# A four-layer decoder trunk in one kernel: the norms between its stages, and one table request, put in another order

## What is computed

```python
for i in range(DEPTH):                       # 2
    hn = rms_norm(h, gains[0])
    mix = retention(hn, ...) if i % 2 == 0 else gated_deltanet(hn, ...)
    h = h + rms_norm(mix, gains[1])
    ff = square(relu(rms_norm(h, gains[2]) @ w_up)) @ w_down      # 1024 -> 4096 -> 1024
    h = h + rms_norm(ff, gains[3])
```

## Time and profile before

| | us |
|---|---|
| median of 3 runs (lowest, highest) | 1483.14 (1481.12, 1483.98) |
| the profiled execution's own time | 1481.87 |
| its span, first instruction to last | 1480.1 |
| TensorE busy | 1453.2 (98%) |
| GpSimd busy | 655.5 (44%) |
| VectorE busy | 591.6 (40%) |
| ScalarE busy | 546.0 (37%) |
| TensorE's granted clock, mean share of full speed | 0.993 |

### The profile page before, as it was taken

How to read it: one execution, slowest core, us unless ns; L and a number is a source line. 1 busy time by engine, 2 the same in 40 slices (tenths; PEclk the granted TensorE clock), 3 DMA queues, 4 the chain that set the end, 5 groups by cost and what they waited for, 6 DMA issues and landing times.

```text
span 1480.1 us, 19872 instructions
## 1 busy us (share of the span) xinstructions
PE 1453.2 (98%) x7772; PEld 1220.5 (82%) x7773; DVE 591.6 (40%) x1095; ACT 546.0 (37%) x1039; POOL 655.5 (44%) x306
## 2 busy tenths in 40 slices
PE   8999999999999999999999999999998999999998
PEld 6988888757889888888888977889988988888886
DVE  3641001264265520044037445797756640024223
ACT  5232243254243222222225457754734322123231
POOL 6245344343544353444447216357435444434442
PEclk9999999999999999999999999999999999999999
DMA  6322322400233223323232222221113132232321
GB/s 220 127 86 85 105 93 88 165 3 29 90 111 116 86 85 103 97 85 114 86 114 86 89 87 86 86 83 35 57 57 129 58 100 99 88 110 87 106 94 57
DMA packets 66557, 136.23 MB, mean 92 GB/s; under 512 B 3632, under 2 KB 4016, under 8 KB 66096
## 3 DMA queue, kind: packets, MB, share of 16 engines
q1 hardware_dynamic: 64016, 125.90, 25.8%
q10 hardware_dynamic: 2464, 9.25, 1.7%
HBM read 133.03 MB, written 2.11 MB: 91 GB/s over the span
## 4 chain that ended last, share of the span: by engine, by line
PE 90%; DVE 4%; ACT 3%; POOL 2%; DMA 1%; issue 1%; DVEq 0%; ACTq 0%; SPq 0%; POOLq 0%
PE bank L452 27%; PE bank L453 27%; PE bank L454 27%; PE bank L660 2%; POOL side_lo L331 1%; PE bank L774 1%; PE bank L646 1%; PE bank L730 1%; POOL w_lo L331 1%; DVE mix L1610 1%; DVE gv L1837 1%; ACT squares L1351 1%; PE bank L499 1%; DVE act_lo L1652 0%; DMA gains<-in_norm_gains_dram 0%
## 5 line engine op out<-in xcount | busy, mean ns | idle before, releaser
L331 POOL TENSOR_TENSOR w_lo<-w_raw,w_hi 128x1024 fp32r<-128x1024 f32 (+1 forms) x218 | 521.5, 2415 | 679.1 <-ACT w_hi L1050 676.2
L1050 ACT ACTIVATE w_hi<-w_raw 128x1024 fp32r<-128x1024 f32 x208 | 209.1, 1055 | 467.1 <-PE bank L454 424.5
L452 PE MATMUL bank<-act_hi,w_hi 128*128 128x512 f32 (+1 forms) x816 | 295.0, 362 | 7.7 <-DVE act_lo L1652 4.4
L454 PE MATMUL bank<-act_hi,w_lo 128*128 128x512 f32 (+1 forms) x816 | 293.3, 359 | 0.0
L453 PE MATMUL bank<-act_lo,w_hi 128*128 128x512 f32 (+1 forms) x816 | 293.2, 359 | 0.0
L453 PE MATMUL bank<-w_lo,hid_hi 128*128 128x512 f32 x480 | 189.0, 394 | 0.0
L452 PE MATMUL bank<-w_hi,hid_hi 128*128 128x512 f32 x480 | 188.2, 392 | 0.0
L454 PE MATMUL bank<-w_hi,hid_lo 128*128 128x512 f32 x480 | 186.4, 388 | 0.0
L452 PEld LDWEIGHTS bank<-act_hi,w_hi 128*128 128x128 f32 x816 | 155.0, 190 | 32.6 <-DVE act_lo L1652 5.5
L1759 DVE TENSOR_TENSOR relu_sq<-relu 128x512 f32<-128x512 f32 x64 | 48.6, 759 | 329.0 <-ACT relu L1076 328.4
L454 PEld LDWEIGHTS bank<-act_hi,w_lo 128*128 128x128 f32 x816 | 155.0, 190 | 22.6
(11 more groups left out here) (280 smaller groups left out, 2169.2 us busy)
## 6 DMA issues: line engine op xcount, KB each, us to landing
w_raw<-in_mlp_w_up_dram SPq DMA_DIRECT2D x32, 1024.0 KB, 5.8
w_raw<-in_mlp_w_down_dram SPq DMA_DIRECT2D x32, 1024.0 KB, 5.0
w_raw<-in_ret_w_in_dram SPq DMA_DIRECT2D x22, 1024.0 KB, 5.1
w_raw<-in_gdn_w_in_dram SPq DMA_DIRECT2D x16, 1024.0 KB, 5.3
w_raw<-in_ret_w_out_dram SPq DMA_DIRECT2D x8, 1024.0 KB, 4.8
w_raw<-in_gdn_w_out_dram SPq DMA_DIRECT2D x4, 1024.0 KB, 5.0
gains<-in_norm_gains_dram ACTq DMA_DIRECT2D x7, 512.0 KB, 6.1
raw_side<-in_ret_w_in_dram SPq DMA_DIRECT2D x2, 1024.0 KB, 15.2
```

Source lines behind the costliest of these rows:

```text
L331: done = nc.gpsimd.tensor_tensor(LO[slot][:, kt, :], RAW[raw][:, kt, :], HI[slot][:, kt, :].bitcast(F32), ALU.subtract)
L452: pe.matmul(dst, sta_hi, mov_hi, start=first, stop=False)
L454: return pe.matmul(dst, sta_lo, mov_hi, start=False, stop=last)
L1050: act.activation(HI[raw if slot is None else slot][:, kt, :], RAW[raw][:, kt, :], ACT.Copy)\
```

## The change

At borders 1 to 3 VectorE makes the low half of tile 0 ahead of the take-out of tile 2, and norms tile 2 ahead of the addition of tile 3 to the residual. At borders 1 and 2 ScalarE splits chunk 2 ahead of the square and root of tile 2's residual. Border 3 gets an order of its own on ScalarE (`norms_of_last_mlp`): the first half of chunk 0 is split ahead of the root of tile 1, the two shares follow one another, and the second half of chunk 0 stands between the high halves of tiles 0 and 1. TensorE turns tile 1 there in the middle of the last group's last part, not behind it. The loop over gate groups is written out, and the decay table is requested ahead of the emptying of the last group. Border 0 is as it was.

```diff
--- before.py
+++ after.py
@@ -453,7 +453,8 @@
                 pe.matmul(dst, sta_hi, mov_lo, start=False, stop=False)
                 return pe.matmul(dst, sta_lo, mov_hi, start=False, stop=last)
 
-            def part(c, j, parity, chunks, m, features_out, a_hi, a_lo, tokens=slice(0, T), fresh=False, slot=None):
+            def part(c, j, parity, chunks, m, features_out, a_hi, a_lo, tokens=slice(0, T), fresh=False, slot=None,
+                     halfway=None):
 
                 hi, lo = HI[j % 2 if slot is None else slot], LO[j % 2 if slot is None else slot]
                 mm = slice(m * P, (m + 1) * P)
@@ -462,6 +463,8 @@
                     if fresh and kt % (CK // 2) == 0:
 
                         pe.wait_ge(w_ready, c * 2 + (2 * j + 1 + kt // (CK // 2)))
+                    if halfway and kt == CK // 2:
+                        halfway()
                     k = j * CK + kt
                     ends = (k == 0, k == chunks * CK - 1)
                     if features_out:
@@ -507,7 +510,8 @@
                 for m, j in ((0, 0), (1, 0), (0, 1), (1, 1), (2, 0), (3, 0), (2, 1), (3, 1)):
                     if (m, j) == (3, 1):
                         turn_tile(norm, 0)
-                    done = part(c, j, 1, 2, m, False, a_hi, a_lo, fresh=m == 0)
+                    done = part(c, j, 1, 2, m, False, a_hi, a_lo, fresh=m == 0,
+                                halfway=(lambda: turn_tile(norm, 1)) if (m, j) == (3, 1) else None)
                     if j:
                         done.then_inc(bank_full, 1)
                     elif m == 3:
@@ -596,8 +600,6 @@
                     turn_tile(b, 0)
                     turn_tile(b, 1)
                     warm_up(8)
-                elif b == 3:
-                    turn_tile(b, 1)
                 pe.wait_ge(sem("act_low"), 2 * (TT * b + 2))
                 for j in range(2):
                     if b == 0 and j == 0:
@@ -1050,6 +1052,12 @@
                     act.activation(HI[raw if slot is None else slot][:, kt, :], RAW[raw][:, kt, :], ACT.Copy)\
                         .then_inc(w_high, 1)
 
+            def split_half(c, slot, half):
+
+                act.wait_ge(w_landed[c % 2], 16 * (c // 2))
+                kt = slice(half * CK // 2, (half + 1) * CK // 2)
+                act.activation(HI[slot][:, kt, :], w_raw[:, c % 2, kt, :], ACT.Copy).then_inc(w_high, 1)
+
             def split_one(c, slot):
 
                 if c in (2, 3):
@@ -1147,8 +1155,36 @@
                 act.wait_ge(chunk_used, u0 + 1)
                 split_one(c0 + 4, 0)
 
+            def norms_of_last_mlp(ready):
+
+                c, slots = FIRST_CHUNK[3], HEAD_SLOTS[3]
+                mix_root(3, 0)
+                mix_root(3, 1)
+                resid_root(3, 0)
+                act.wait_ge(chunk_used, ready)
+                split_half(c, slots[0], 0)
+                resid_root(3, 1)
+                norm_share(3, 0)
+                norm_share(3, 1)
+                high_acts(3, 0)
+                split_half(c, slots[0], 1)
+                high_acts(3, 1)
+                mix_root(3, 2)
+                act.wait_ge(bank_full, 4 * NEXT_GROUP[3])
+                head_splits(3, 1, 2)
+                mix_root(3, 3)
+                resid_root(3, 2)
+                head_splits(3, 2, 3)
+                resid_root(3, 3)
+                head_splits(3, 3, 4)
+                high_acts(3, 2)
+                high_acts(3, 3)
+
             def norms(b, ready):
 
+                if b == 3:
+                    norms_of_last_mlp(ready)
+                    return
                 mix_root(b, 0)
                 mix_root(b, 1)
                 resid_root(b, 0)
@@ -1172,14 +1208,16 @@
                         kt = slice(m * CK // 2, (m + 1) * CK // 2)
                         act.activation(HI[0][:, kt, :], w_raw[:, 0, kt, :], ACT.Copy).then_inc(w_high, 1)
                 mix_root(b, 2)
-                if b == 3:
-                    act.wait_ge(bank_full, 4 * NEXT_GROUP[b])
                 head_splits(b, 1, 2)
                 mix_root(b, 3)
-                resid_root(b, 2)
                 if b == 2:
                     act.wait_ge(bank_full, 4 * NEXT_GROUP[b])
-                head_splits(b, 2, 3)
+                if b:
+                    head_splits(b, 2, 3)
+                    resid_root(b, 2)
+                else:
+                    resid_root(b, 2)
+                    head_splits(b, 2, 3)
                 resid_root(b, 3)
                 head_splits(b, 3, 4)
                 high_acts(b, 2)
@@ -1216,13 +1254,12 @@
                     for m in range(4):
                         empty(RET_V, i, p, m, v_tm[:, m, bass.ds(i * GC, GC)])
             act.wait_ge(sem("roped"), KT)
-            with act.Fori(0, 2) as i2:
-                for p in range(2):
-                    i = i2 * 2 + p
-                    splits(RET_G, i, 2)
-                    for m in range(4):
-                        empty(RET_G, i, p, m, gate[:, m, bass.ds(i * GC, GC)], ACT.Silu)
-            act.dma_start(decay[:, :, :], decay_c).then_inc(sem("decay_landed"), 16)
+            for i in range(4):
+                splits(RET_G, i, 2)
+                if i == 3:
+                    act.dma_start(decay[:, :, :], decay_c).then_inc(sem("decay_landed"), 16)
+                for m in range(4):
+                    empty(RET_G, i, i % 2, m, gate[:, m, i * GC:(i + 1) * GC], ACT.Silu)
             act.wait_ge(sem("gate_gained"), 4 * TT)
             load_gains(1)
             splits(RET_OUT, 0, 4, last=1)
@@ -1669,16 +1706,18 @@
                     return
                 norm_tile(b, 0)
                 norm_tile(b, 1)
+                low_acts(b, 0)
                 if b:
                     take_out(b, 1, 2, more)
-                low_acts(b, 0)
                 low_acts(b, 1)
                 if b:
                     take_out(b, 1, 3, more)
-                    for m in (2, 3):
-                        mix_rstd(b, m)
-                        add_mix(b, m)
+                    mix_rstd(b, 2)
+                    add_mix(b, 2)
+                    mix_rstd(b, 3)
                 norm_tile(b, 2)
+                if b:
+                    add_mix(b, 3)
                 norm_tile(b, 3)
                 low_acts(b, 2)
                 low_acts(b, 3)
```

## The result

The changed kernel takes 1488.76 us (median of 6 runs, 1488.04 to 1489.45) beside 1483.43 for the kernel before (6 runs, 1481.12 to 1483.98): ratio 1.0042, 95% interval 1.0032 to 1.0052, slower by 5.3 us. The forecast was 1490.1, range 1485 to 1494. The profiled execution has a span of 1486.3 us, 6.2 more than before; the difference of the medians is the better measure of the time, the profiled executions are used to say where it goes.

The account below looks back on a forecast made before the run. TensorE, busy 1453.2 of 1480.1 us, was taken to bound the kernel. Table -1.8, borders 1 to 3 +1.7, +1.9, +1.7, and clock +3.5 summed to +7.0 on the 1483.14 median: 1490.1 us, range 1485 to 1494.

Parts of the forecast that it names:

- Decay table: In retention, before the second block of scores: the earlier request removes TensorE's 1.64 us wait and some overlap, -1.8 us.
- next late is TensorE itself: Behind the decay product in retention: no other hole follows up to 345 us, so the full -1.8 us is kept.
- Border 1: Retention into MLP 0: TensorE stands 1.2 us ahead of tile 2 and 2.7 ahead of tile 3, +1.7 us.
- Border 2: MLP 0 into DeltaNet: three small waits go, one 4.1 us stall opens ahead of tile 3, +1.9 us.
- Border 3: Ahead of MLP 1: the 3.48 us wait shrinks to some 0.7, waits of 2.0 and 4.1 open, +1.7 us.
- The race for the port: At tile 3, GpSimd beats VectorE by under 0.1 us; if VectorE wins, each border costs 0.5 us less.
- The clock: Behind the 4.1 us stalls at borders 2 and 3 it falls, 0 to 2.6 us each, 1.7 taken: +3.5 us.
- the likeliest case: The forecast itself, with clock falls behind the stalls at borders 2 and 3: 1486.6 to 1492 us, chance 0.55.
- Rival A: The holes ahead of tile 3 open but the clock stays up: +3.5 us, 1486.6; chance 0.15.
- Rival C: The decay table wins nothing, or the clock also falls at border 1: +8.8 to +9.6, up to 1493; chance 0.14.
- Rival B: VectorE and GpSimd do not clash at the new places, the waits close: -11.5 us, 1471.6; chance 0.10.

Follow-up runs that it names:

- Kernel 1: The kernel before with only the decay table requested ahead of the last gate group's emptying (loop written out): 1480.12 us beside 1482.52, ratio 0.9980.
- kernel 7: The changed kernel with 18, 30 and 30 unread matmuls added ahead of tile 3's turn at borders 1, 2 and 3: 1484.41 us, ratio 1.0015.
- kernel 5: The changed kernel with GpSimd's subtractions for the first four chunks of borders 1 to 3 cut in two: 1484.27 us, ratio 1.0012.
- kernel 6: The changed kernel with GpSimd clears replacing its subtractions for the first four chunks of borders 1 to 3, low halves missing: 1471.05 us, ratio 0.9924.
- kernel 2: The changed kernel with VectorE's add of tile 3 put back ahead of the norm of tile 2: 1485.31 us, ratio 1.0020.
- kernel 4: The changed kernel with VectorE's order of tile 3 and ScalarE's early split both undone: 1478.71 us, ratio 0.9970.
- kernel 8: As kernel 4, with GpSimd's subtractions for the second chunk of borders 1 to 3 cut in two: 1476.40 us, ratio 0.9956.
- kernel 3: The changed kernel with ScalarE's root of tile 2 put back ahead of chunk 2's split at borders 1 and 2: 1494.54 us, ratio 1.0087.

## Why the prediction was right, point by point

**Sign, mechanism and size held.** +5.3 us measured, +7.0 foretold. The profiled execution shows +6.1, so 0.8 of the miss of 1.7 is only which executions were profiled, and the terms below account for the other 0.9.

- *Decay table*, -1.8: the ledger has -2.1 at border 1, less the -0.15 that was there at border 0, so -1.95. Kernel 1 gives -2.4 by its median. The step "next late is TensorE itself" held.
- *Border 1*, +1.7 with stalls of 1.2 and 2.7: the ledger has +1.85, the rows 1.27 and 2.77. *Border 2*, +1.9 with one stall of 4.1: +1.85 and 4.15. Its steps came one by one, all 0.7 us earlier as the turn of tile 0 was: the norm of tile 2 ended at 801.94 (802.6 foretold), the add of tile 3 at 806.17 (806.9), GpSimd took the fourth chunk at 808.71 (809.4). *Border 3*, +1.7 with 2.0 and 4.1: from +3.1 at the turn of tile 0, 0.5 of which is that turn's own slip, to +4.5: about +1.9, with 1.89, 0.48 and 4.34. I had left the 0.48 out.
- *The race for the port* was named as undecided by under 0.1 us. GpSimd won it at all three borders, by 0.08, 0.07 and 0.08 us.
- *The clock*, +3.5, was the mis-sized term, and it is the one that had only bounds. It fell after both of the long stalls, as the likeliest case had it; a fall costs less than the 1.7 taken: 16 matmuls of 256 columns at 0.21 instead of 0.12 us make 1.5. The two together are 3.1 by the traces, and kernel 7 puts them at 2.8 by the medians (5.3 less 2.5). The one fall I had a row of slowed 28 matmuls, and a single case says little of the next. By the rule of the Trainium skill (page "TensorE: Matmul & The Clock Gate", section "Why this matters for your kernels"), that idle gaps between bursts of matmuls bring the half rate back, with the full price of that row, I had estimated +8.7; the trace agrees that both long stalls are followed by a fall, and the price was smaller.
- *Rival A* (no fall) is out by the clock rows. *Rival C* (a third fall, at border 1) stayed away by luck more than by anything I could have known: the 2.77 us stall there was followed by none, kernel 5's of 2.88 at the same place was. *Rival B* (no clash, -11.5) was rightly given little, and kernel 6, with the low halves left out, comes near its price: -10.9.
- *What was not foretold:* 0.4 us won inside MLP 0 in the changed kernel (-0.25 to -0.7 in the ledger). TensorE shows no wait in that stretch in either trace. The gain lies in 96 matmuls, the late half of chunks 2 and 3: 11.3 us before and in kernels 1, 2, 4, 5 and 8, 10.9 in the changed kernel and in kernels 3, 6 and 7. Its cause stays open. The part of the loss between borders 2 and 3 (+1.15 to +3.1) is the fall of the clock (1.5) and the slip of tile 0's turn (0.5).

## What to carry to other kernels

Before an instruction is pulled ahead, list what now stands behind it on its own queue, and follow that one to TensorE: here two moves that each freed a tile or a chunk sooner made the next tile later by more. Test such moves in all four combinations: ScalarE's early split cost 6.6 us with VectorE's old order and saved 6.7 with the new one. Where VectorE and GpSimd both read two tiles of SBUF, write down who issues first at each meeting; a meeting costs up to the length of one GpSimd instruction, and cutting it in two on the critical chunk alone made tile 2's add 1.2 us shorter at border 3. Add a possible fall of the clock to the price of each stall: here about 1.5 us behind each stall of 4.

## What the runs showed of the hardware that I had not expected

A clear on GpSimd that only writes does not hold a VectorE step with two SBUF inputs: 0.75 us each in kernel 6 with GpSimd clearing beside them, against 2.91 beside a subtraction. I had used that only for the two clears of border 2. The Trainium skill (page "SBUF — State Buffer", section "Who interferes with whom") says so too, that such a step contends with a GpSimd instruction that reads SBUF and not with one that only writes it; the trace agrees.

A fall of the granted clock has no fixed price: behind the 4.15 us stall of the changed kernel it slowed 16 matmuls (1.5 us), behind the 3.48 us stall of before 28 (2.6 us), behind the same 3.48 us in kernel 1 about 18. Nor do the lengths tell a fall from none: in the profiled executions one followed each stall of 3.48 us or more, and also those of 2.88 and 2.41 (kernel 5), 2.30 (kernel 2), 2.29 (kernel 4) and 1.90 (kernel 7), but not those of 2.77 and 1.89 (the changed kernel) or 1.91 (kernel 3). And filling an idle stall with matmuls whose result nobody reads won 2.8 us by the medians, within about 2 either way, with nothing else changed; each of kernel 7's 11 executions (1486.49 at most) was faster than each of the changed kernel's 6 (1488.04 at least), though the two did not run side by side.
